# Experts' weights in pairs: one 2 MB transfer into two neighbouring ring slots instead of two of 1 MB

## The reference

```python
logits = t @ w_router                                # t: 256 x 1024, 8 experts
top_vals, top_idx = lax.top_k(logits, 2)
gates = sum(one_hot(top_idx, 8) * softmax(top_vals)[..., None], axis=1)
for e in range(8):
    h = silu(t @ w_gate_e[e]) * (t @ w_up_e[e])      # 1024 x 3584 each
    out = out + gates[:, e:e + 1] * (h @ w_down_e[e])  # 3584 x 1024
```

## Time and profile before

| | |
|---|---|
| median of 3 runs | 2476.16 us (2476.04 to 2476.7) |
| the profiled execution | 2479.77 us |
| its span, first to last instruction | 2477.9 us |
| mean granted TensorE clock | 0.996 of full speed |
| PE busy | 2451.2 us, 99% |
| PE weight loads busy | 2042.5 us, 82% |
| DVE busy | 1851.6 us, 75% |
| ACT busy | 1553.5 us, 63% |
| POOL busy | 35.3 us, 1% |
| DMA | 637.96 MB, mean 257 GB/s |
| chain of work that ended last | 93% PE, 3% DVE, 2% ACT, 1% DMA |

### The profile page before, as it was taken

How to read it: one execution, slowest core, us unless ns; L and a number is a source line. 1 busy time by engine, 2 the same in 40 slices (tenths; PEclk the granted TensorE clock), 3 DMA queues, 4 the chain that set the end, 5 groups by cost and what they waited for, 6 DMA issues and landing times.

```text
span 2477.9 us, 30459 instructions
## 1 busy us (share of the span) xinstructions
PE 2451.2 (99%) x12032; PEld 2042.5 (82%) x12032; DVE 1851.6 (75%) x1862; ACT 1553.5 (63%) x1896; POOL 35.3 (1%) x36
## 2 busy tenths in 40 slices
PE   8999999999999999999999999999999999999998
PEld 8788888897887889978888897888888888888886
DVE  6877744478675546645554478999999999999998
ACT  5675543457465444365443447788778787878886
POOL 1000000000000000010000001000000000000001
PEclk9999999999999999999999999999999999999999
DMA  7444655454345564675654556999999999999996
GB/s 251 152 136 153 221 182 171 135 174 159 104 162 208 205 212 154 198 261 178 227 179 174 177 190 268 404 363 406 369 398 374 402 377 385 391 383 396 377 389 254
DMA packets 183223, 637.96 MB, mean 257 GB/s; under 512 B 11196, under 2 KB 52594, under 8 KB 139914
## 3 DMA queue, kind: packets, MB, share of 16 engines
q1 hardware_dynamic: 179562, 622.87, 68.1%
q0 software_dynamic: 3488, 12.59, 1.3%
HBM read 616.54 MB, written 18.88 MB: 256 GB/s over the span
## 4 chain that ended last, share of the span: by engine, by line
PE 93%; DVE 3%; ACT 2%; DMA 1%; issue 1%; SPq 0%; DVEq 0%; ACTq 0%
PE bank L561 89%; PE bank L598 2%; DVE split L2150 2%; PE bank L905 2%; DMA ring<-in_moe_w_gate 1%; ACT split L1536 1%; ACT parts L1536 0%; PE bank L1457 0%; DVE parts L2130 0%; DVE parts L2219 0%; DVE oT_high L2164 0%; ACT L1536 0%; DMA const<-in_tables 0%; DVE x_resid L2192 0%; DVE tmp L2207 0%
## 5 line engine op out<-in xcount | busy, mean ns | idle before, releaser
L561 PE MATMUL bank<-split,parts 128*128 128x512 f32 (+1 forms) x6432 | 1467.7, 388 | 7.1 <-DVE split L2150 2.2
L561 PEld LDWEIGHTS bank<-split,parts 128*128 128x128 f32 x6432 | 1186.3, 188 | 255.1 <-issue 16.0
L1536 ACT ACTIVATE split<-ring 128x2048 fp32r<-128x2048 f32 x444 | 848.6, 1922 | 442.7 <-PE bank L561 405.4
L2150 DVE TENSOR_TENSOR split<-ring,split 128x2048 fp32r<-128x2048 f32 x444 | 994.3, 2283 | 59.1 <-ACT split L1536 58.8
L2219 DVE TENSOR_TENSOR parts<-bank,parts 128x512 fp32r<-128x512 f32 x128 | 82.4, 686 | 157.5 <-ACT parts L1536 156.1
L1536 ACT ACTIVATE halves<-ring 128x1024 fp32r<-128x1024 f32 x96 | 101.0, 1061 | 129.9 <-PE bank L561 129.4
L2164 DVE TENSOR_TENSOR halves<-ring,halves 128x1024 fp32r<-128x1024 f32 x96 | 116.2, 1224 | 73.0 <-ACT halves L1536 72.3
L561 PE MATMUL bank<-ring_low,z_high 128*128 128x512 f32 (+2 forms) x384 | 146.8, 382 | 0.0
L561 PE MATMUL bank<-xparts,halves 128*128 128x256 f32 x960 | 116.4, 283 | 0.0
L561 PEld LDWEIGHTS bank<-xparts,halves 128*128 128x128 f32 x960 | 115.5, 192 | 0.5 <-DVE xparts L2130 0.2
L561 PE MATMUL bank<-z_high 128*128 128x512 f32 (+3 forms) x304 | 111.0, 365 | 0.0
(11 more groups left out here) (345 smaller groups left out, 2346.8 us busy)
## 6 DMA issues: line engine op xcount, KB each, us to landing
ring<-in_moe_w_gate SPq DMA_DIRECT2D x112, 1024.0 KB, 8.4
ring<-in_moe_w_up SPq DMA_DIRECT2D x112, 1024.0 KB, 7.9
ring<-in_moe_w_down SPq DMA_DIRECT2D x112, 1024.0 KB, 8.0
ring<-in_w_gate_up SPq DMA_DIRECT2D x44, 1024.0 KB, 5.8
ring<-in_w_in SPq DMA_DIRECT2D x40, 1024.0 KB, 5.3
ring<-in_ret_w_in SPq DMA_DIRECT2D x24, 1024.0 KB, 5.3
ring<-in_w_down SPq DMA_DIRECT2D x22, 1024.0 KB, 7.1
ring<-in_w_in SPq DMA_DIRECT2D x20, 880.0 KB, 4.9
```

The costliest lines, as they stand in the source:

```text
L561: return nc.tensor.matmul(o, l, r, start=first, stop=final, **kw)
L1536: return nc.scalar.activation(out, in_, func, **kw)
L2150: V.tensor_tensor(split[:, split_place(m), 1, :], ring[:, n % RING, :], split[:, split_place(m), 0, :].bitcast(F32), ALU.subtract).then_in ...
```

## The change

The host lays an expert's weights out so that the two units of a gate, up or down part are neighbours in each partition's row: 16 KB per partition, 2 MB in one block. A new `stream_pair` waits until both old units of the two slots have been read, issues one transfer that fills slots n and n + 1, and counts it on the even slot's semaphore alone. Readers of either unit wait for that semaphore. Order, ring size, splits and all computing instructions are as before.

```diff
+        def pair_of(n):
+
+            return n - n % 2
+
...
-                    eng.wait_ge(loaded[n % RING].sem, 16 * (n // RING + 1))
+                    held = pair_of(n) if m >= dense_splits else n
+                    eng.wait_ge(loaded[held % RING].sem, 16 * (held // RING + 1))
...
-            final = len(unit_read) - 1
+            final = pair_of(len(unit_read) - 1)
...
+            def stream_pair(src):
+
+                nonlocal n
+                assert n % 2 == 0 and RING % 2 == 0
+                for held in (n, n + 1):
+                    sig, value = unit_read[held - RING]
+                    eng.wait_ge(sig.sem, value)
+                eng.dma_start(ring[:, n % RING:n % RING + 2, :], src).then_inc(loaded[n % RING].sem, 16)
+                n += 2
...
-                            for kh in range(2):
-                                stream(a[name][e, i, kh], (1, UNIT))
+                            stream_pair(a[name][e, i])
                     if i:
-                        for r in range(2):
-                            stream(a["moe_w_down_2"][e, 2 * (i - 1) + r], (1, UNIT))
+                        stream_pair(a["moe_w_down_2"][e, i - 1])
...
-        w = arrays[name].reshape(NE, 2, 4, P, GROUPS, HALF).transpose(0, 4, 1, 3, 2, 5)
-        arrays[name] = np.ascontiguousarray(w).reshape(NE, GROUPS, 2, P, UNIT)
-    w = arrays["moe_w_down_2"].reshape(NE, 2 * GROUPS, 2, P, D).transpose(0, 1, 3, 2, 4)
-    arrays["moe_w_down_2"] = np.ascontiguousarray(w).reshape(NE, 2 * GROUPS, P, UNIT)
+        w = arrays[name].reshape(NE, 2, 4, P, GROUPS, HALF).transpose(0, 4, 3, 1, 2, 5)
+        arrays[name] = np.ascontiguousarray(w).reshape(NE, GROUPS, P, 2, UNIT)
+    w = arrays["moe_w_down_2"].reshape(NE, GROUPS, 4, P, D).transpose(0, 1, 3, 2, 4)
+    arrays["moe_w_down_2"] = np.ascontiguousarray(w).reshape(NE, GROUPS, P, 2, UNIT)
```

## The result

The changed kernel takes 2542.01 us (median of 4 runs, 2539.18 to 2544.61) against 2476.43 us before, measured beside it: ratio 1.0259, 95% interval 1.0247 to 1.0271, so 65.6 us slower. The direction was forecast, the size was not: 2494 us had been said, with a range up to 2514. The profiled execution took 2540.45 us, with a span of 2538.6 us, 60.7 us longer than before.

A forecast was written before the change was run, and what follows sets the result against it. PE was taken as the bound, busy 2451.2 of 2477.9 us. Landing together 15.7 plus both slots free 2 made 18 us on the profiled 2479.77, 2498; as that execution stood 3.6 above the median, 2494 us, range 2481 to 2514.

The forecast's parts named there:

- unit 16: Counting an expert's 42 units from 0, the one queued behind row store and token load; the one place where landings count.
- Landing together: Before unit 16, a pair's first unit lands with its second, 2.49 us later; 15.7 us over eight experts.
- Both slots free: Units 12 to 17: pair issued when second old unit is read; 0.3 us in each of six experts, 2 us.
- the holes: Times ahead of unit 16 when the old queue waited for slots; most of the late start's shift was to fall there.
- The ring of three pairs, nothing lost: Quiet, ring-limited stretches: a 2 MB load lands in 7.2 us, upper bound 10.6; slack 0.4 us for ACT, no loss.
- rival C: Ring loop binds everywhere: with 9 us transfers, rounds exceed PE's 16.8 us; +28 us beside 16, 2520 us; chance 0.12.
- PE's matmuls and DVE's subtractions keep their durations: A sign for the profile after: these instructions take as long as before; no added time forecast for them.
- Edges: Stage's first and final pairs: uncovered, each end would cost 2.5 us, 5 us in all; taken as nothing.
- A: Rival, hidden: the pair's lateness is absorbed by slack; costs 0 to 4 us, 2476 to 2480; chance 0.12.
- B: Rival: larger rows and fewer completions speed the backlogged queue about 10% above 421 GB/s; 2473 us; chance 0.04.
- The signs to look for: Near unit 16 only: PE idle grows 1.4 to 3 us per expert, ACT waits near 5 us; minimum landing near 7.2.

The follow-up runs named there:

- the late issue: Kernel before, 1 MB transfers with single landings, but SP issues a pair's two transfers back to back once both old slots were read: 2499.18 us, ratio 1.0081.
- the 12 fillers: Changed kernel plus 12 useless filler products in each expert, ahead of the transposes where PE idles before unit 16: 2577.61 us, ratio 1.0391.

## Why the prediction was wrong, step by step

- *PE sets the time, SP waits for DVE, unit 16 is the place where landings count.* Right. The three longest of PE's waits in the experts' stage of the changed kernel are there.
- *Landing together, 15.7 us.* Right in place, mechanism and roughly in size: alone it makes PE wait 18.9 us there, against 0.8 before, and costs 0.83%, 21.6 us.
- *Both slots free, 0.3 us in each of six experts.* Mis-sized. I had bounded it by 0 and 2.5 us and chosen next to nothing, "because of the holes" in the old queue. Alone it costs 18.8 us and makes PE wait 16.7 us in seven experts, 15.9 more than before: 2.3 us each, near the upper bound. Expert 1 shows how much the holes took, with times counted from PE's transposes. The issue of units 12 and 13, before and with the late issue:

```profile
1642.65 0.60 PE L905 MATMUL bank<-const,tmp 128*128 128x128 f32 x4
1643.84 4.09 SPq L2971 DMA_DIRECT2D ring<-in_moe_w_up  x2
```

```profile
1638.26 0.60 PE L905 MATMUL bank<-const,tmp 128*128 128x128 f32 x4
1643.24 0.80 SPq L2977 DMA_DIRECT2D ring<-in_moe_w_up  x2
```

  Unit 12 is issued 4.98 us behind the transposes and not 1.19, so 3.8 us later. ACT starts unit 16 at 1666.16, 13.83 us behind the next transposes (1652.33), and not 11.65 (1668.37 from 1656.72), so 2.2 us later. The holes took 1.6 us of the shift, not most of it.
- *The ring of three pairs, nothing lost.* This is the step that failed. I took 7.2 us to landing, from the best case of one unit, 4.7, plus 2.5. The right row was the ring-limited stretch itself, which I had not read for this. The ring's transfers of the kernel before in 1717 to 1745 us:

```profile
DMA to landing us min/median/max: 4.8/6.9/7.9
```

  There is little backlog there, yet the median is 6.9 us; that it is so because units are issued 2.2 us after each other is my reading, which no run tests. 6.9 + 2.5 = 9.4 us would have been close to the 9.8 measured over the stage. In the same stretch of the changed kernel its four pairs take more still, near the 10.6 us that I had named as the upper bound:

```profile
DMA to landing us min/median/max: 9.2/10.3/10.9
```

  My own rival C set a round of 14.9 to 16.2 us at 7.2 us against PE's 16.8. At 9.8 it is 17.5 to 18.8, at 10.3 it is 18.0 to 19.3: the loop can bind, and in expert 1 PE's round from 1715.55 to 1733.51 took 17.96 us where it had taken 16.78 (1708.24 to 1725.02). The sum does not say by how much: 0.7 to 2.0 us in each of 49 rounds would be 34 to 98 us, and the changed kernel has 15 such waits in experts 1 to 7, 15.3 us. C had a chance of 0.12 and I had put aside the median of 8.1 as "made of backlog". Its 2520 us came nearer than the forecast, in part by luck: its 28 us for the ring were more than the 15.3 measured, its 16 us for unit 16 less than the 24.8, and it had nothing for the busy time either.
- *The busy time.* No step had it; I wrote that "PE's matmuls and DVE's subtractions keep their durations". It grew by 15.2 us, by 20.3 us without the slow 10 us of the old execution. At most 12.7 us are the clock, which is at its lower level for 3.4 or 6.8 us with some of the long stalls, and about 8 us the matmul runs that waits break up, both estimates from above. I had counted a stall of PE at its idle time alone. The Trainium skill, "TensorE: Matmul & The Clock Gate", section "HAM oscillation — how this bites in real kernels", tells of waits for DMA between groups of matmuls after which the array starts slow again. The trace agrees in most places, 4.23 us idle before 1680.28 and then a granted clock of 0.50, but not in all: 3.48 us idle before 1938.48 left it at 1.00.
- *Edges.* Expert 0 was given 1.4 us. The 45.5 us of added idle time less 24.8 us at unit 16 (25.6 - 0.8) and 15.3 us elsewhere leave 5.4 us. In 1520 to 1620 us, the time of expert 0, PE waits 5.7 us where it waited 1.0, which is 4.7 of them.
- *Rivals.* A fell: no stall was absorbed. B fell, as in the backlog of expert 1 the pairs are moved no faster (before, after):

```profile
1656.00:1680.00 24.00, 23.54 (x108) 19.13 (x106) 20.79 (x15) 17.80 (x15) 0.00 (x0) 1.00 1.02 422
```

```profile
1656.00:1680.00 24.00, 19.36 (x86) 15.35 (x85) 17.21 (x14) 13.58 (x11) 0.00 (x0) 1.00 1.01 403
```

- *The signs to look for* were right for unit 16 (ACT's wait "near 5 us": 5.20), but PE's idle time of 1.4 to 3 us per expert was too low (3.7). PE idle in several groups was named as the sign of C, and it is there. The minimum landing was said to be near 7.2 us and was 7.9.

Summed by the profiles: 24.8 us waiting at unit 16, 15.3 us in the ring's other tight places, 5.4 us for expert 0 and the rest, 15.2 us of busy time: 60.7 us, the difference of the two spans. The forecast had 16.3, nothing, 1.4 and nothing for these. So the two terms put at nothing, the ring and the busy time, make 30.5 of the 43 us that were missing, and unit 16 another 8.5.

## What to carry to other kernels

Joining two transfers of a ring makes the first wait for the second twice, once for a free slot and once for the landing, and both stand in the same round trip, where their costs did more than add. Work out that round (issue, landing, every reader) with a landing time read in a stretch where the ring really is the limit, not with the best case of one transfer; a stage whose PE is busy at 99% may be two slots away from a steep loss. A stall of a few us can cost more than its length, because the clock may fall with it; and where two extra transfers stand in a weight stream, try them apart.

## What the runs showed of the hardware that I had not expected

- In this queue 1 MB transfers issued behind each other already moved 421 GB/s; those of 2 MB brought nothing (403 GB/s in the backlog of expert 1, where it had been 422). Rows of 16 KB and of 8 KB gave 1.0259 and 1.027.
- In the experts' stage of the changed kernel no 2 MB transfer landed in under 7.9 us, though a single megabyte took 4.7 at best and each one behind it 2.5.
- The granted clock fell after idle times of PE of 4.23 us and (in the stretch at 1981 us) 2.38 us in the changed kernel, but not after 3.48 us at 1938.48 us in the same execution. The length of the stall alone doesn't tell.
- The same code far from the change, at 645 us, ran for 10.2 us at the lower clock in one profiled execution and at full clock in the other. Two single profiles can differ by 5 us for such a reason.
- A product with a float32 stationary and moving operand took 2 x 0.43 us (24 matmuls of the 12 fillers start from 1680.7 to 1690.6 us) where a pass of the fp32r kind takes 0.23 us (2.79 us for 12).
